# Attention: a head's turned-block copies between the exponentials; recurrence: operands made inside a wait; three stage ends rearranged

## What is computed

```python
c = split_cols(h @ w_in + b_in)
S_a, oa = scan_stream(gla_block, s_gla, (qa, ka, va, la))          # gated linear attention, 4 heads
conv_out = silu(causal_conv(qk_pre, s_conv, conv_w, conv_b))       # 4 taps, on 512 columns
qb, kb = conv_out[..., :W_B], conv_out[..., W_B:] * DH_B ** -0.5
(C_b, n_b, m_b), hb = scan_stream(mlstm_block, (s_c, s_n, s_m), (qb, kb, vb, ig, lf))
yc = dsa_prompt(...)     # the 256 best keys of each query by an indexer's score, then softmax attention, 8 heads
y = concatenate([ya, yb, yc]) @ w_out
h = layer_norm(ALPHA * h + y);  h = layer_norm(ALPHA * h + moe(h))
return h, (k_new, v_new, ki_new, S_a, C_b, n_b, m_b, conv_buf)     # rows and states are outputs too
```

## Time and profile before

| | |
|---|---|
| median of 3 runs | 1391.04 us (1385.22 to 1391.98) |
| profiled execution | 1385.14 us, span 1383.3 us |
| mean granted TensorE clock | 0.904 |
| PE / PEld busy | 1201.9 us (87%) / 663.8 us |
| DVE / ACT / POOL busy | 681.0 / 447.5 / 419.6 us |
| projection ends | 469.3 us |
| recurrence | 469.3 to 634.9 us |
| attention | 634.9 to 836 us |
| output projection, routing, experts | 836 to 1383.3 us |

### The profile page before, as it was taken

The page is one execution under the profiler, slowest core; times in us unless marked ns, Lnnn a source line. Parts: engine busy times, 40 slices in busy tenths (PEclk is TensorE's granted clock), DMA queues, the critical chain, the costliest instruction groups (busy, mean ns, idle before and its releaser), DMA issues. The chain is left out here.

```text
span 1383.3 us, 18207 instructions
## 1 busy us (share of the span) xinstructions
PE 1201.9 (87%) x5971; PEld 663.8 (48%) x5972; DVE 681.0 (49%) x1861; ACT 447.5 (32%) x845; POOL 419.6 (30%) x469
## 2 busy tenths in 40 slices
PE   4899999999998268896978899999839999999990
PEld 3455655455554146684655584555533333333330
DVE  7115699999992055524645522222561322222227
ACT  6224100211111322203666531111315444444417
POOL 0001021106388522105876005442111333333210
PEclk9999899999999557766999999999759999999995
DMA  9300000011010200004000004532714798968445
GB/s 369 144 16 1 1 1 1 0 31 31 31 45 0 65 0 1 1 3 153 1 1 2 1 1 175 193 135 95 273 31 143 208 280 292 330 208 273 87 132 204
DMA packets 35774, 136.92 MB, mean 99 GB/s; under 512 B 9658, under 2 KB 12266, under 8 KB 30842
## 3 DMA queue, kind: packets, MB, share of 16 engines
q1 hardware_dynamic: 28218, 108.79, 21.2%
q0 software_dynamic: 7488, 27.27, 8.4%
HBM read 101.24 MB, written 34.80 MB: 98 GB/s over the span
## 5 line engine op out<-in xcount | busy, mean ns | idle before, releaser
L439 PE MATMUL p<-hT,p_wfm 128*128 128x512 f32 (+1 forms) x624 | 207.4, 495 | 2.1 <-PEq L106 2.1
L2166 PE MATMUL p_G<-p_wgu,p_xT 128*64 x416 | 186.2, 601 | 0.4 <-ACT p_xT L2091 0.4
L2168 PE MATMUL p_G<-p_high_gu,p_xT 128*64 128x512 f32 x416 | 186.2, 601 | 0.0
L453 PE MATMUL p<-p_wtm,hT 128*128 128x399 f32 (+1 forms) x480 | 165.6, 504 | 0.0
L439 PEld LDWEIGHTS p<-hT,p_wfm 128*128 128x128 f32 x624 | 105.7, 192 | 104.1 <-issue 104.1
L453 PEld LDWEIGHTS p<-p_wtm,hT 128*128 128x128 f32 (+1 forms) x480 | 85.6, 180 | 77.4 <-issue 14.6
L1987 POOL DMA_INDIRECT sum_rows<-p_ys,p_dest_of x26 | 55.4, 2131 | 199.1 <-DVE p_ys L2028 199.1
L2101 ACT COPY p_high_gu<-p_wgu 128x1024 f32 x104 | 101.0, 1042 | 39.8 <-issue 36.8
L583 DVE TENSOR_SCALAR_CACHE_REDUCE key_bias<-p_score,p_trial 128x272 bf16<-128x272 f32 (+4 forms) x155 | 108.4, 759 | 1.1
L1367 DVE CUSTOM_DVE_ANT_0 p_logit<-p_L,key_bias 128x272 f32<-128x272 f32 (+6 forms) x120 | 56.9, 500 | 105.2 <-PE p_L L1435 81.0
L2166 PEld LDWEIGHTS p_G<-p_wgu,p_xT 128*64 128x64 f32 x416 | 55.3, 138 | 110.5 <-issue 110.5
(11 more groups left out here) (454 smaller groups left out, 2075.3 us busy)
## 6 DMA issues: line engine op xcount, KB each, us to landing
p_wgu<-in_w_gu SPq DMA_DIRECT2D x16, 2048.0 KB, 9.4
p_wd<-in_w_down SPq DMA_DIRECT2D x16, 1024.0 KB, 12.3
p_wfm<-in_w_fm SPq DMA_DIRECT2D x13, 512.0 KB, 3.7
p_wtm<-in_w_tm SPq DMA_DIRECT2D x8, 598.5 KB, 15.7
p_x<-in_x SPq DMA_DIRECT2D x9, 512.0 KB, 9.4
h_rows<-p_x SPq DMA_DIRECT2D x9, 512.0 KB, 14.8
p_h<-h_rows SPq DMA_DIRECT2D x9, 512.0 KB, 3.3
h_rows<-p_h SPq DMA_DIRECT2D x9, 512.0 KB, 2.7
```

What stands on the lines that cost most here:

```text
L439: mm = nc.tensor.matmul(ps[3 * u + c][:, 0:b - a], w[:, u, k, :], m.hT[:, k, a:b], start=k == 0, stop=k == KD - 1)
L453: mm = nc.tensor.matmul(bank["tokens", n][0:rows, 0:TG], stream, m.wtm[:, k, g * TG:(g + 1) * TG], start=k == 0, stop=k == KD - 1)
L2166: nc.tensor.matmul(pG[u][low, :], xT[:, u, k, low], wgu[:, ds(slot, 1), k, :].rearrange("p a n -> p (a n)"), start=k == 0, stop=k == KD - 1)
L2168: mm = nc.tensor.matmul(pG[u][high, :], xT[:, u, k, high], high_gu[:, u, k, :], start=k == 0, stop=k == KD - 1)
```

## The change

Seven edits in three stages.

1. Projection, ACT: the features before the Silus are 6; 7 and 8; 9 and 10; 11 and 12, instead of 6 and 7; 8 and 9; 10 and 11; 12.
2. Projection, POOL to DVE: the two key features are scaled by DVE behind its last tie, each behind its Silu.
3. Projection, SP: the three row transfers of v go before the wait for the fourth convolution; those of k and the indexer keys go into the recurrence, behind its loads; the recurrence waits for all nine at its end.
4. Recurrence, DVE: `operands(t + 2)` stands inside `totals(t)`, between the scaling and the wait for L1173.
5. Recurrence, SP: the transfers of `C0` and `nlast` leave the stage; `nlast` moves to another place in SBUF.
6. Attention, SP and ACT: the same data are sent first thing in this stage, as four transfers over 128 partitions instead of eight over 64; ACT waits for them before its first copy of pair 1.
7. Attention, ACT: step p is exponential of head 0 of pair p, copies of head 0 of pair p - 1, exponential of head 1, copies of head 1.

```diff
+def rows_to(sp, m, d, name, landed):
+    c, width = {"k": (CK, 128), "v": (CV, 128), "kidx": (CI, DI)}[name]
+    out = d["p_" + name]
+    sp.dma_start(out[0:META, :], m.tm[0:META, MT, c:c + width]).then_inc(landed, 16)
+    sp.dma_start(out[META:PROMPT, :].rearrange("(j p) c -> p j c", p=P), m.tm[:, 0:NT, c:c + width]).then_inc(landed, 16)
+    sp.dma_start(d["s_" + name], m.tm[:, SAMPLE, c:c + width]).then_inc(landed, 16)
...
 # phase_project, SP
+                sp.wait_ge(bias_added, len(groups))
+                rows_to(sp, m, d, "v", m.rows_out)
                 sp.wait_ge(acc_ready, 4)
...
                 sp.wait_ge(conv_out, 32)
-                sp.wait_ge(bias_added, len(groups))
-                sp.wait_ge(rows_copied, TT + 1)
...
-                sp.wait_ge(rows_out, 16 * n)
 # phase_project, POOL
-                for c in range(2):
-                    pool.wait_ge(silu_ready, 3 + c)
-                    g.tensor_scalar(m.fm[:, F_BK + c, :], m.fm[:, F_BK + c, :], DHB ** -0.5, None, ALU.mult).then_inc(keys_scaled, 1)
 # phase_project, ACT
                 for c in range(4):
-                    for u in range(2 if c < 3 else 1):
-                        feature_tile(F_BK // 2 + c, u)
+                    for k in range(F_BK + max(2 * c - 1, 0), F_BK + 2 * c + 1):
+                        feature_tile(k // 2, k % 2)
                     act.wait_ge(acc_ready, c + 1)
 # phase_project, DVE
                 first_ties()
+                for c in range(2):
+                    dve.wait_ge(silu_ready, 3 + c)
+                    nc.vector.tensor_scalar(m.fm[:, F_BK + c, :], m.fm[:, F_BK + c, :], DHB ** -0.5, None, ALU.mult).then_inc(keys_scaled, 1)
 # phase_recurrent, SP
                 sp.dma_start(C0[:, :, :, :], d["mlstm_state"]).then_inc(c0_in, 16)
+                rows_to(sp, m, d, "k", m.rows_out)
+                rows_to(sp, m, d, "kidx", m.rows_out)
...
-                sp.wait_ge(m_done, 1)
-                sp.wait_ge(n_copied, 1)
-                for p, e in every_two:
-                    put(d["s_c"][2 * p + e, :, :, :], C0[m_rows(e), p, :, 0:DVA])
-                    put(d["s_n"][2 * p + e, :, :], nlast[m_rows(e), p, :])
                 sp.wait_ge(out, 16 * n)
+                sp.wait_ge(m.rows_out, 16 * 9)
 # phase_recurrent, DVE, in totals(t)
+                    if t + 2 < TT:
+                        operands(t + 2)
                     dve.wait_ge(num_ready, t + 1)
 # phase_recurrent, DVE, the loop over t
                     output(t)
-                    if t + 2 < TT:
-                        operands(t + 2)
 # phase_dsa, SP
+                for p in range(2):
+                    sp.dma_start(d["s_c"][2 * p:2 * p + 2, :, :, :].rearrange("e k i v -> (e k) i v"), m.C0[:, p, :, 0:DVA]).then_inc(m.states_out, 16)
+                    sp.dma_start(d["s_n"][2 * p:2 * p + 2, :, :].rearrange("e k i -> (e k) i"), m.nlast[:, p, :]).then_inc(m.states_out, 16)
                 sp.dma_start(g[:, :, :], d["g_norms"].partition_broadcast(P)).then_inc(g_in, 16)
 # phase_dsa, ACT, in copies(g)
+                    if g == 2:
+                        act.wait_ge(m.states_out, 16 * 4)
 # phase_dsa, ACT, the loop over p
                     for i in range(2):
                         if p < NP:
                             exponent(2 * p + i)
-                    for i in range(2):
                         if p:
                             copies(2 * p - 2 + i)
```

More of the change, by code:

```diff
@@ L151, in phase_norm_in @@
         m.wtm_in, m.normal_out = nc.alloc_semaphore("p2_wtm_in"), nc.alloc_semaphore("p2_normal_out")
+        m.rows_out = nc.alloc_semaphore("p4_rows_out")
         rows_of = lambda t: P if t < TT else META
@@ L327, in phase_project @@
         w_in = [sem("w_in0"), sem("w_in1")]
-        (rows_out, kiC_in, fm_ready, fm_copied, tm_ready, tm_copied, bias_added, zeroed, qiz_ready,
+        (kiC_in, fm_ready, fm_copied, tm_ready, tm_copied, bias_added, zeroed, qiz_ready,
          raw_ready, relu_ready, relu_used, dve_own, round_own, conv_in, pool_own, acc_ready, silu_ready, keys_scaled, conv_out, rows_ready, rows_copied) = (sem(n) for n in (
-            "rows_out kiC_in fm_ready fm_copied tm_ready tm_copied bias_added zeroed qiz_ready "
+            "kiC_in fm_ready fm_copied tm_ready tm_copied bias_added zeroed qiz_ready "
             "raw_ready relu_ready relu_used dve_own round_own conv_in pool_own acc_ready silu_ready keys_scaled conv_out rows_ready rows_copied").split())
@@ L369, in _ @@
                 sp.wait_ge(conv_out, 32)
-                sp.wait_ge(bias_added, len(groups))
-                sp.wait_ge(rows_copied, TT + 1)
-                n = 0
-                for name, c, width in (("k", CK, 128), ("v", CV, 128), ("kidx", CI, DI)):
-                    out = d["p_" + name]
-                    sp.dma_start(out[0:META, :], m.tm[0:META, MT, c:c + width]).then_inc(rows_out, 16)
-                    sp.dma_start(out[META:PROMPT, :].rearrange("(j p) c -> p j c", p=P),
-                                   m.tm[:, 0:NT, c:c + width]).then_inc(rows_out, 16)
-                    sp.dma_start(d["s_" + name], m.tm[:, SAMPLE, c:c + width]).then_inc(rows_out, 16)
-                    n += 3
-                sp.wait_ge(rows_out, 16 * n)
             @block.gpsimd
@@ L638, in phase_recurrent @@
         sem = Semaphores(nc, "p4_")
+        sem.made += [m.rows_out]
         VE = DVA + 1
@@ L648, in phase_recurrent @@
         S0, C0 = al("S0", [P, NSEQ, DVA]), al("C0", [P, 2, NSEQ, VE])
-        kdT, kw = al("kdT", [P, 2, P]), al("kw", [P, 2, 256])
+        kdT, kw, nlast = al("kdT", [P, 2, P]), al("kw", [P, 2, 256]), al("nlast", [P, 2, NSEQ])
+        m.C0, m.nlast, m.states_out = C0, nlast, nc.alloc_semaphore("p6_states_out")
         al = Bump(m, "p4_", m.SCR, m.END - TT * 1024 - BIAS_BYTES)
@@ L659, in phase_recurrent @@
         m0r, m0t = al("m0r", [P, NSEQ]), al("m0t", [P, HB])
-        slb, nlast = al("slb", [P, 2, 16]), al("nlast", [P, 2, NSEQ])
+        slb = al("slb", [P, 2, 16])
         mids, exm, kdm, rel_s, last_s = al("mids", [P, 3, NT + 1]), al("exm", [P, META]), al("kdm", [P, META]), al("rel_s", [P, P]), al("last_s", [P, P])
@@ L1227, in phase_dsa @@
         sem = Semaphores(nc, "p6_")
+        sem.made += [m.states_out]
         GQ = HC // KVC
@@ L1285, in _ @@
                 sp.dma_start(m.w_out2[:, :, :], d["w_out"][:, 2:6, :]).then_inc(w_in, 16)
+                sp.wait_ge(m.states_out, 16 * 4)
                 sp.wait_ge(caches_in, 32)
```

## The result

| | before | after |
|---|---|---|
| median | 1388.13 us (4 runs, 1384.54 to 1391.98) | 1335.43 us (4 runs, 1334.35 to 1339.26) |
| ratio, 95% interval | | 0.9625 (0.9587 to 0.9663) |
| span of the profiled execution, granted clock | 1383.3 us, 0.904 | 1337.2 us, 0.917 |

A forecast was written before the change was run, and what follows sets the result against it. Bound by each fenced stage's path: POOL and SP at the projection's end, TensorE's gaps and clock in the recurrence, TensorE in attention. Terms -20.0 - 22 - 6.9 - 7.6 = -56.5 gave 1328.6; forecast 1332 us, range 1323 to 1349.

The forecast's parts named there:

- Projection: Projection's end: earlier Silus and convolutions, key scaling on DVE, row transfers moved; recurrence starts at 449.3, -20.0 us (-16 to -21).
- the fourth: Projection: POOL's fourth convolution starts at 416.7, loses some 2.4 us to DVE and ends at 443.2.
- Recurrence, its loop: Recurrence tiles: operands made in DVE's wait close TensorE's gaps, no clock fall until the sample tile; -22 us (-8 to -24).
- Rival (a): Recurrence: density of the work, not idle gaps, decides the clock; -8.8 instead of -22, about 1345 us; chance 0.22.
- rival (d): Recurrence: operands don't fit the wait because ACT's exponentials come later than the products; 1356 us; chance 0.05.
- Recurrence, its end: Recurrence's end: state transfers move into the attention, which starts at 627.95; -6.9 us (-6 to -7.2).
- Attention: Attention: copies between exponentials shorten TensorE's waits, net -6.2; with the shorter wait at tile 5, -7.6 us (-3 to -11).
- Rival (c): Attention: later second-head copies make TensorE wait before the values, deciding above 1.6 us a pair; about 1450 us; chance 0.03.
- (b): Attention's order and POOL's projection chain give half; 1343 us with the clock held, 1356 without; chance 0.13.
- the signs that I had named: Recurrence from about 449, clock full from second tile; attention some 49 us earlier, its 28 waits about 10 us in total.

The follow-up runs named there:

- e6: The changed kernel with the recurrence's operands waiting only for the first three exponentials: 1334.05 us, ratio 0.9604.
- e7: The changed kernel with attention copies between the exponentials only where heads have two groups of blocks (tiles 3 to 6): 1329.11 us, ratio 0.9568.
- e5: The kernel before with eight needless matmuls in each of the seven gaps before the recurrence's scores: 1372.35 us, ratio 0.9874.
- e2: The kernel before with only the recurrence's operands made inside DVE's wait: 1362.78 us, ratio 0.9809.
- e4: The kernel before with only the transfers moved, rows into the recurrence and states into the attention: 1376.16 us, ratio 0.9929.
- e3: The kernel before with only the projection's Silu order changed and the key scaling moved to DVE: 1376.52 us, ratio 0.9909.
- e9: The changed kernel with POOL making the sample tile's masked values ahead of the keys of tile 2: 1333.86 us, ratio 0.9637.
- e10: The changed kernel with copies interleaved only for two-group heads, operands waiting for three exponentials, and masked values made early: 1334.63 us, ratio 0.9636.
- e11: The changed kernel without DVE's tie breaking in the projection, so the attention weights other keys: 1331.58 us, ratio 0.9615.

## Why the prediction came out as it did

**Projection: -20.0 forecast, -17.6 measured** (-18.4 as the mean of four executions: the change twice, e6 and e7). The chain was right: Silus, convolutions and transfers moved as worked out, and the third convolution took 33.7 us where the earlier trace rows have 33.6. The mis-sized term is the fourth. I took 26.5 us for it, with 2.4 lost to DVE in the overlap; it took 28.5 and lost 4.3, since what runs in those last 7 us are DVE's longest operations. Laid to the 7.1 us of overlap with the ties, the 4.3 us mean that POOL kept about 0.4 of its rate (an estimate), where I had bounded it at 0.6 to 0.8. It also started 1 us later, with the third. The Silu then came at 446.3, not 443.6. The scaling on DVE delayed nothing behind it, as I said; it ran 0.95 us beside POOL and 0.77 alone. What it cost POOL can't be told apart from the 4.3 us. The 1 us for it, by the Trainium skill's rule on the shared port pair ("SBUF — State Buffer", "Who interferes with whom"), was not in my sum.

**Recurrence, its loop: -22 forecast, -16.8 measured.** Mechanism right: the seven gaps went and the clock had no more falls from them. Rival (a), density, is refuted for the loop by e5 and e2, though it holds in the sample tile; rival (d) is out as well, the operands fit. Two terms were too good. First, I let the clock be full from the second tile on, since that is where the profile before had it. The rise comes 42 to 71 us into the stage in the executions of the change and its variants; in the one compared it came at 67.5, so that two tiles took 12.3 and 10.7 us instead of 10.9 and 6.95, together 5.2 us. Second, the tile takes 7.17 us, not 6.95: 0.9 us in five tiles. The reason stood in the earlier trace rows and I read past it: L836 costs 0.29 us there because it runs alone, while in its new place it is released by the same exponential as POOL's product. The stretch behind the loop took 0.5 us less, and my sum had rounded 22.3 to 22; that leaves the 5.2 us. The four executions with the old loop took 153.7 us on average, the six with a period of 7.17 took 137.6: -16 is the fair size of this term, as the profile of before was on the slow side (143.8 to 162.4).

**Recurrence, its end: -6.9 forecast, -6.8 measured**, and the moved transfers were hidden by more than I had allowed.

**Attention: -7.6 forecast, -4.3 measured.** The waits fell nearly as worked out: 0.71 instead of 1.13 in tile 3, 1.41 instead of 2.21 at tile 5 with no fall of the clock behind it, and the price in tiles 1, 2 and 7 is the one that e7 takes back (2.9 us). The sum of the waits fell by 8.1; I had 9.6 for the second heads alone. What fell short was the base: in the profile of before the clock was full 13 us into the attention, and in the thirteen other executions after 16 to 26. Compared at the same point the order gives 6.8, without the fall at tile 5. That fall is not the rule, as I had taken it to be: of the five executions with the old order, all with the wait of 2.21 us there, before, e4 and e5 have it, e2 and e3 don't. In e4 and e5, with the clock full after 21 us as in e2, the stage is 2.1 and 2.3 us longer than in e2, which is the price of it; I had put it at 1.8. The wait and the clock behind it, in before and in e2:

```profile
717.72 0.84 PE L1454 MATMUL p_P<-const,p_logit 128*128 128x128 f32 x6 [2.21 <-ACT p_pT L1404]
719.00:720.00 1.00, 1.00 (x6) 0.55 (x4) 0.13 (x1) 0.30 (x2) 1.00 (x2) 0.51 0.00 0
...
699.00 0.85 PE L1454 MATMUL p_P<-const,p_logit 128*128 128x128 f32 x6 [2.21 <-ACT p_pT L1404]
700.00:702.00 2.00, 2.00 (x20) 1.17 (x20) 1.10 (x5) 0.58 (x2) 1.92 (x3) 1.00 0.00 0
```

**The stages behind: 0 forecast, -0.6 measured.** The misses are 2.4 + 5.2 + 0.1 + 3.3 - 0.6, together 10.4: 1383.3 - 56.5 would have been 1326.8, and the span is 1337.2. The median missed by 3.4 us only, and part of that is luck. The profiled execution of the change, at 1339.26 us, was the slowest of its four, 3.8 above their median; and I had added 3.4 us to the profiled execution's value for the spread of before. Most of that spread did go: 18 runs of before lay within 17 us (1376.4 to 1393.1), eight of the change within 8 (1331.1 to 1339.3).

Rival (c), the wait before the values, was real but small: 2.1 us in seven waits of at most 0.4 (before: 0.6 in three), far from the 1.6 us a pair at which it would decide. Of (b), the half that concerns POOL's chain happened in part. Of the signs that I had named, three didn't come: the clock was not full from the second tile, the attention began 41 us earlier and not 49, and its 28 waits total 14.1 us and not about 10; from 22.2 and my own 9.6 it should have read 12.6.

## What to carry to other kernels

Where TensorE works in a loop with one short idle stretch a turn, look at its clock before pricing that stretch: here gaps of 8.8 us held 16 to 22 us in the traces (26 by the medians), and even dummy work in them paid. When an operation moves to another place, take its duration from the row only if what runs beside it stays the same; what is released by the same event will run beside it. Before comparing a stage of two executions, compare when the clock rose in each; a difference of several us may lie there and not in the edit.

## What the runs showed of the hardware

- **POOL's product holds DVE's operation to its own end.** 0.15 us became 2.37 (L929), 0.23 became 3.59 (L860), 0.29 became 0.58 (L836). All three read their inputs from SBUF. In the first execution of the change the same 3.60 us product lay beside DVE operations that read one input from PSUM (503.59 to 507.19), and they kept their lengths: L918 took 0.43 us, L925 two times in 0.48. The Trainium skill, "SBUF — State Buffer", section "Who interferes with whom", states this: a DVE instruction with two SBUF inputs contends with a GpSimd one that reads SBUF, and the pair is an exclusive lock. The runs agree; I had used the rule for the projection and not for the tile. In these rows it doesn't help that the DVE operation is small: it ends when POOL's product does, or up to 0.15 us behind it.
- **The clock fell in loops whose TensorE idled 1.4 us a tile**, 12 times in four executions, and not once, between the rise and the sample tile, in six without such gaps and without a wait of over 2 us there (the change, e2, e5, e9, e10, e11). At one wait of 2.15 to 2.5 us at full clock in these two stages it fell in seven of nine executions, during the wait or within 2 us of its end: four of four in the loop, three of five at tile 5 of the attention. So such a wait makes a fall likely, not certain.
- **It also fell with TensorE busy**, in the sample tile, in fourteen of fourteen executions, among products of 0.12 us on 32 rows; in the 3 us ahead of the fall TensorE shows as busy for 2.94 to 3.00 us.
- **When it first rises differs from execution to execution of one kernel**: 43 and 67.5 us into the same stage in the two executions of the change. What decides it stays open.
